# A 10-stage transformer kernel on one core: the first stage's norm factor is applied to the gate and up banks instead of to x, and two modulation groups move to the fourth feed-forward stage

## What is computed

```
def rmsnorm(x, g):
    x32 = x.astype(jnp.float32)
    y = x32 * lax.rsqrt(jnp.mean(x32 * x32, axis=-1, keepdims=True) + RMS_EPS)
    return (y * g.astype(jnp.float32)).astype(x.dtype)

def swiglu(x, w_in, w_out):
    gate, up = jnp.split(x @ w_in, 2, axis=-1)
    return (jax.nn.silu(gate) * up) @ w_out

x = x + 0.5 * swiglu(rmsnorm(x, ffn1_norm_g[l]), ffn1_w_in[l], ffn1_w_out[l])   # first stage
c_act = jax.nn.silu(c)
mod = c_act @ mod_w[i] + mod_b[i]                                               # 18 groups of 1024 columns
```

## Time and profile before

| | |
|---|---|
| median of 3 runs | 1636.75 us |
| the profiled execution | 1635.02 us |
| its span, first to last instruction | 1633.3 us (1.7 us lie outside) |
| PE busy | 1619.9 us, 99% |
| DVE busy | 1190.6 us, 73% |
| ACT busy | 802.6 us, 49% |
| mean granted TensorE clock | 0.996 |
| mean DMA rate over the span | 223 GB/s |

### The profile page before, as it was taken

How to read it: one execution, slowest core, us unless ns; L and a number is a source line. 1 busy time by engine, 2 the same in 40 slices (tenths; PEclk the granted TensorE clock), 3 DMA queues, 4 the chain that set the end, 5 groups by cost and what they waited for, 6 DMA issues and landing times.

```text
span 1633.3 us, 33769 instructions
## 1 busy us (share of the span) xinstructions
PE 1619.9 (99%) x14172; PEld 1592.6 (98%) x14172; DVE 1190.6 (73%) x1348; ACT 802.6 (49%) x887; POOL 48.1 (3%) x81
## 2 busy tenths in 40 slices
PE   9999999999999999999999999999999999999998
PEld 9999999999999999999999999999999998899998
DVE  6888876676788888888877788847655578774544
ACT  5444557554544445434457654445444456654442
POOL 0000000000000000000000000000000001000000
PEclk9999999999999999999999999999999999999999
DMA  8998845344489885988743368754555535445551
GB/s 334 340 335 322 309 155 181 137 159 154 172 299 327 325 331 192 329 332 296 271 155 130 141 222 323 268 194 151 203 203 183 202 130 185 152 155 195 192 192 65
DMA packets 51063, 365.02 MB, mean 223 GB/s; under 512 B 5792, under 2 KB 5920, under 8 KB 7072
## 3 DMA queue, kind: packets, MB, share of 16 engines
q1 hardware_dynamic: 40320, 287.04, 48.0%
q0 software_dynamic: 10368, 75.50, 12.9%
q10 hardware_dynamic: 288, 1.18, 0.2%
HBM read 362.65 MB, written 1.05 MB: 223 GB/s over the span
## 4 chain that ended last, share of the span: by engine, by line
PE 95%; DVE 3%; ACT 1%; issue 1%; DVEq 0%; ACTq 0%
PE bank L258 53%; PE bank L294 26%; PE bank L250 3%; PE bank L277 3%; PE bank L374 1%; PE bank L1817 1%; PE bank L385 1%; DVE wlo L189 1%; PE bank L2228 0%; PE bank L419 0%; PE bank L1324 0%; PE bank L1863 0%; PE bank L1769 0%; PE bank L1787 0%; PE bank L815 0%
## 5 line engine op out<-in xcount | busy, mean ns | idle before, releaser
L189 DVE TENSOR_TENSOR wlo<-raw,whi 128x2048 fp32r<-128x2048 f32 x253 | 578.7, 2288 | 220.0 <-ACT whi L181 219.8
L258 PE MATMUL bank<-xh,whi 128*128 128x256 f32 x2608 | 724.8, 278 | 0.7 <-DVE wlo L189 0.7
L258 PE MATMUL bank<-xl,whi 128*128 128x256 f32 x2608 | 721.4, 277 | 0.0
L258 PE MATMUL bank<-xh,wlo 128*128 128x256 f32 x2608 | 721.3, 277 | 0.0
L181 ACT ACTIVATE whi<-raw 128x2048 fp32r<-128x2048 f32 x253 | 483.6, 1914 | 308.0 <-PE bank L258 190.8
L258 PEld LDWEIGHTS bank<-xh,whi 128*128 128x128 f32 x2608 | 490.5, 188 | 2.2 <-DVE wlo L189 0.9
L258 PEld LDWEIGHTS bank<-xl,whi 128*128 128x128 f32 x2608 | 489.9, 188 | 0.1
L258 PEld LDWEIGHTS bank<-xh,wlo 128*128 128x128 f32 x2608 | 489.7, 188 | 0.0
L294 PE MATMUL bank<-hid_hi,whi 128*128 128x256 f32 x1056 | 291.9, 276 | 0.0
L294 PE MATMUL bank<-hid_hi,wlo 128*128 128x256 f32 x1056 | 291.5, 276 | 0.0
L294 PE MATMUL bank<-hid_lo,whi 128*128 128x256 f32 x1056 | 291.5, 276 | 0.0
(11 more groups left out here) (349 smaller groups left out, 1737.5 us busy)
## 6 DMA issues: line engine op xcount, KB each, us to landing
raw<-stream_in SPq DMA_DIRECT2D x269, 1024.0 KB, 4.9
mod_raw<-mod_in POOLq DMA_DIRECT2D x72, 1024.0 KB, 7.2
params<-params_in SPq DMA_DIRECT2D x1, 1474.0 KB, 14.3
x<-x_in SPq DMA_DIRECT2D x2, 512.0 KB, 4.5
raw<-stream_in SPq DMA_DIRECT2D x2, 512.0 KB, 6.6
m_gsu<-sgu_in ACTq DMA_DIRECT2D x1, 1024.0 KB, 6.9
y_out<-x SPq DMA_DIRECT2D x4, 256.0 KB, 2.6
consts<-consts_in SPq DMA_DIRECT2D x1, 280.5 KB, 6.3
```

Source lines behind the costliest of these rows:

```text
L189: dve.tensor_tensor(wlo[:, s, :], raw[:, s, :], whi[:, s, :].bitcast(F32), ALU.subtract)\
L258: last = pe.matmul(out[:, m, :], (whi, wlo)[wp][:, s, k * 256 + m * P:k * 256 + m * P + P], (xh, xl)[ap][:, k, :], start=(k == 0 and j == ...
```

## The change

Ffn 0 gets its own code (`FACTOR_LATER`). x is no longer multiplied by the norm's factor. ACT rounds x times gain for tiles 0 to 3, and DVE for tiles 4 to 7 (`xh`), as x lands, and DVE takes the remainders. Block 0 goes whi with xh, whi with xl, and wlo with xh last. Gate and up of step 0 go to two accumulator banks that are free then. The squares are summed behind block 1 by one matmul against ones (`pe_mean_squares`), which leaves the sum on all partitions. The root and the reciprocal are taken on 128x256 instead of 128x2. Each gate bank is multiplied by the factor on DVE (`scale_gate`) ahead of Silu, and each up bank likewise (first instruction of `post`), which are two more DVE instructions of 128x512 per step. The gains are loaded on ACT's queue, the masks are made later, and there are 78 dummy matmuls at the start instead of 70, and none in the first norm. `MOD_GROUPS` becomes 3, 5, 5, 5, and in ffn 0 the groups stand in turns 1 to 3 of 0 to 4. Some semaphores are merged, with no change to an order.

```
+FACTOR_LATER = (0,)
-MOD_GROUPS = {0: 5, 1: 5, 2: 5, 3: 3, 4: 0, 5: 0}
+MOD_GROUPS = {0: 3, 1: 5, 2: 5, 3: 5, 4: 0, 5: 0}
...
+                for k in range(4):
+                    act.activation(xh[:, k, :], x[:, k, :], ACT.Identity, scale=g[:, k:k + 1]).then_inc(sem("xn_rounded"), 2)
...
+        def dve_first_remainders(dve):
+            g = prm(GAIN_OF[0])
+            dve.wait_ge(sem("gain_loaded"), 16)
+            for k in range(2):
+                dve.wait_ge(sem("xn_rounded"), 2 * k + 2)
+                dve_remainder(dve, 0, k)
+            dve.wait_ge(sem("x_loaded1"), 16)
+            for k in range(4, 8):
+                dve.tensor_scalar(xh[:, k, :], x[:, k, :], g[:, k:k + 1], None, ALU.mult).then_inc(sem("xn_ready"), 1)
+                if k < 6:
+                    dve.wait_ge(sem("xn_rounded"), 2 * k - 2)
+                    dve_remainder(dve, 0, k - 2)
+            for k in range(4, 8):
+                dve.wait_ge(sem("xn_ready"), k - 3)
+                dve_remainder(dve, 0, k)
...
+        def dve_fold_squares(dve, n):
+            i = N_PAIRS * pair_index[n]
+            dve.wait_ge(sem("x_squared"), X_STEPS * norm_index[n] + X_STEPS)
+            for step, w in enumerate((4, 2, 1)):
+                if step:
+                    dve.wait_ge(sem("x_paired"), i + step)
+                dve.tensor_tensor(xm[:, 0:w, :], xm[:, 0:w, :], xm[:, w:2 * w, :], ALU.add)\
+                   .then_inc(sem("x_paired"), 1 if step < 2 else N_PAIRS - 2)
+        def pe_mean_squares(pe, n):
+            pe.wait_ge(sem("x_paired"), N_PAIRS * pair_index[n] + N_PAIRS)
+            pe.matmul(STAT[:, 0:T], ones, xm[:, 0, :], start=True, stop=True, skip_group_check=True).then_inc(sem("x_summed"), 1)
...
+        def pe_first_block(pe, out):
+            s = slot_of(0)
+            for part, (w, xs) in enumerate(((whi, xh), (whi, xl), (wlo, xh))):
+                if part == 2:
+                    pe.wait_ge(sem("w_lo_ready"), 1)
+                for k in range(KD):
...
+                    if part == 0 and k == 4:
+                        pe.wait_ge(sem("w_hi_ready"), 1)
+                    if part == 0:
+                        pe.wait_ge(sem("xn_rounded" if k < 4 else "xn_ready"), 2 * k + 2 if k < 4 else k - 3)
+                    if part == 1:
+                        pe.wait_ge(sem("xn_split"), k + 1)
+                    for m in range(2):
...
+        def pe_ffn_later(pe, n, f, groups):
...
+                pe_first_block(pe, pair(ACC[0]))
...
+            pe_in(pe, F0 + 1, pair(ACC[1]))
+            pe_mean_squares(pe, n)
+            def turn(i, first):
+                for q in range(2):
+                    b = F0 + 2 + 3 * q
+                    if not (first and q == 0):
+                        pe.wait_ge(sem("bank_scaled"), L0 + 1 + 2 * q + 4 * i)
+                    pe_in(pe, b, pair(GATE), i, 6)
+                    if first and q == 0:
...
+                        pe_apart(pe, STAT[:, 0:P])
+                    else:
+                        pe.wait_ge(sem("bank_scaled"), L0 + 2 + 2 * q + 4 * i)
+                    pe_in(pe, b + 1, pair(UP), i, 6)
+                    pe.wait_ge(sem("hid_split"), S0 + 1 + q + 2 * i)
+                    pe_out(pe, b + 2, hid_hi[:, q], hid_lo[:, q], first and q == 0, False, i, 6)
...
+            pe_out(pe, F0 + 32, hid_hi[:, 0], hid_lo[:, 0], False, True, between=lambda: pe_mod_fold(pe, n, f, groups))
...
+        def act_ffn_later(act, n, f):
...
+            act_rounded_gain(act, n)
+            if n == 0:
+                act.wait_ge(sem("w_loaded_part"), 16)
+                act.activation(whi[:, 0, 0:H], raw[:, 0, 0:H], ACT.Copy).then_inc(sem("w_half_ready"), 1)
+                act.wait_ge(sem("w_loaded0"), 16)
+                act.activation(whi[:, 0, H:BLK], raw[:, 0, H:BLK], ACT.Copy).then_inc(sem("w_hi_ready"), 1)
+                act_squares(act, 0)
+                act_split(act, 1)
+                act.wait_ge(sem("x_loaded1"), 16)
+                act_squares(act, 1)
+                act_split(act, 2)
...
+            act_split(act, F0 + 3)
+            act_root(act, n)
+            act_split(act, F0 + 4)
+            def silu(s, i=0, ps=0):
+                act.wait_ge(sem("bank_scaled"), L0 + 2 * s + 1 + 2 * ps * i)
+                act.activation(gate[:, :, :], gate[:, :, :], ACT.Silu).then_inc(sem("silu_done"), 1)
...
+            silu(0)
+            round_hidden(0, 0)
...
+            def turn(i, first):
+                for q in range(2):
+                    b = F0 + 2 + 3 * q
+                    if not (first and q == 0):
+                        act_split(act, b + 2, i, 6)
+                    act_split(act, b + 3, i, 6)
+                    silu(1 + q, i, 2)
+                    round_hidden(1 + q, (1 + q) % 2, i, 2)
+                    act_split(act, b + 4, i, 6)
...
+            dve_split(dve, F0 + 3)
+            dve_factor(dve, n)
+            def scale_gate(s, src, block, i=0, per=0, ps=0):
+                dve.wait_ge(sem("w_used"), block + 1 + per * i)
+                if s > 0:
+                    dve.wait_ge(sem("hid_ready"), S0 + s + ps * i)
+                dve.tensor_tensor(gate[:, :, :], src, over(rstd[:, :], [P, 2, T]), ALU.mult).then_inc(sem("bank_scaled"), 1)
+            def post(s, src, block, parity, i=0, per=0, ps=0, between=None):
+                dve.wait_ge(sem("w_used"), block + 1 + per * i)
+                if s > 0:
+                    dve.wait_ge(sem("hid_split"), S0 + s + ps * i)
+                dve.tensor_tensor(hid[:, :, :], src, over(rstd[:, :], [P, 2, T]), ALU.mult).then_inc(sem("bank_scaled"), 1)
+                dve.wait_ge(sem("bank_scaled"), L0 + 2 * s + 2 + 2 * ps * i)
+                dve.wait_ge(sem("silu_done"), S0 + s + 1 + ps * i)
+                dve.tensor_tensor(hid[:, :, :], hid[:, :, :], gate[:, :, :], ALU.mult).then_inc(sem("hid_ready"), 1)
+                if between is not None:
+                    between()
+                dve.wait_ge(sem("hid_rounded"), S0 + s + 1 + ps * i)
+                dve.tensor_tensor(hid_lo[:, parity], hid[:, :, :], hid_hi[:, parity].bitcast(F32), ALU.subtract)\
+                   .then_inc(sem("hid_split"), 1)
+            scale_gate(0, pair(ACC[0]), F0)
+            post(0, pair(ACC[1]), F0 + 1, 0, between=lambda: dve_split(dve, F0 + 4))
...
+            def turn(i, ahead, with_mod, first=False):
...
+                for q in range(2):
+                    b, step = F0 + 2 + 3 * q + 6 * ahead, 1 + q + 2 * ahead
+                    if with_mod:
+                        mod_block(2 * q, g0, i)
+                    if not (first and q == 0):
+                        dve_split(dve, b + 2, i, 6)
+                    scale_gate(step, pair(GATE), b, i, 6, 2)
+                    if with_mod:
+                        mod_block(2 * q + 1, g0, i)
+                    dve_split(dve, b + 3, i, 6)
+                    post(step, pair(UP), b + 1, (1 + q) % 2, i, 6, 2)
+                    dve_split(dve, b + 4, i, 6)
+                    if with_mod and q == 1:
+                        mod_sum(g0, i)
+            turn(0, 0, False, True)
+            with dve.Fori(0, groups) as i:
+                turn(i, 1, True)
...
-            sp.dma_start(params[:, 0:4 * KD], a_params[:, 0:4 * KD]).then_inc(sem("consts_loaded"), 16)
...
-            for _ in range(70):
+            for _ in range(78):
...
+            act.dma_start(params[:, 0:4 * KD], a_params[:, 0:4 * KD]).then_inc(sem("gain_loaded"), 16)
...
-            for p in range(N_PAIRS):
-                dve_pair(dve, 0, p)
...
```

More of the change, by code:

```diff
@@ L412, in pe_norm @@
             if n == 0:
-                pe.wait_ge(sem("consts_loaded"), 32)
+                pe.wait_ge(sem("consts_loaded"), 16)
                 pe.wait_ge(sem("masks_ready"), 3)
@@ L487, in build_program @@
         pair_index = {n: i for i, n in enumerate(n for n in norm_index if n != AFTER_FINAL)}
+        spread_index = {n: i for i, n in enumerate(n for n in norm_index if n not in FACTOR_LATER)}
+        later_index = {n: i for i, n in enumerate(FACTOR_LATER)}
         split_index = {}
@@ L577, in pe_ffn @@
             pe.wait_ge(sem("hid_split"), S0 + STEPS)
-            pe_out(pe, F0 + 32, hid_hi[:, 0], hid_lo[:, 0], False, True, between=mod_fold if groups else None)
+            pe_out(pe, F0 + 32, hid_hi[:, 0], hid_lo[:, 0], False, True, between=(lambda: pe_mod_fold(pe, n, f, groups)) if groups else None)
+        def pe_first_block(pe, out):
[3 more added lines that the diff above has]
+                    pe.wait_ge(sem("w_lo_ready"), 1)
+                for k in range(KD):
+                    if part == 0 and k == 0:
+                        pe.wait_ge(sem("w_half_ready"), 1)
+                    if part == 0 and k == 4:
[5 more added lines that the diff above has]
+                    for m in range(2):
+                        c = k * 256 + m * P
```

(40 more changed lines are left out.)

145 lines of the change are left out of this document (117 added, 28 removed).

## The result

The changed kernel took 1636.43 us, the median of 22 executions (1633.03 to 1642.89), against 1634.92 (1631.47 to 1636.94) of the kernel before. The ratio is 1.0016, 95% interval 1.0009 to 1.0024: 2.6 us slower, which is measurable but inside the 0.2% that I called no change. That closeness is part luck: my number was the kernel before plus 0.15, with 1636.75 for the kernel before, the median of 3 executions, and over 22 that median is 1.8 us lower. The executions do not lie round it, though. With 12 more from a later comparison, 23 of 34 lie between 1633.0 and 1638.2 (median 1636.0) and 11 between 1640.2 and 1643.4 (median 1641.8), with nothing between. The kernel before shows no such second level: its highest in these two comparisons (22 and 35 executions) is 1639.6.

The account below looks back on a forecast made before the run. PE, busy 1619.9 of 1633.3 us, bounds the kernel. Block 4 -0.2, landings -0.2, end of ffn 0 -0.15, end of ffn 3 +0.7 make +0.15 on 1635.02; with 1.73 to the median, 1636.9 us, no change, range 1635.0 to 1639.2.

Parts of the forecast that it names:

- Up to block 3: Start of ffn 0: block 1 at about 17.2, block 2 ending 3.4 us earlier, block 3 at 30.67, gain 1.3 us.
- The landings: DMA queues at the start: moving the gains to ACT's queue lands weights earlier, 0.2 us gained, bounds 0 and 0.5.
- Block 4: First output block: step 0's longer chain lets PE start it at 37.3 against 37.51, 0.2 us gained.
- DVE's turns: First stage: a turn with a group takes 34.3 us against PE's 32.64; the reserve covers it, cost 0.
- Ends of stages: Column sums: end of ffn 0 gains 0.15 us, end of ffn 3 loses 0.7.
- From there on PE works without a break in both kernels: From block 4 on: PE never waits as long as DVE keeps up.
- Rival B: Pauses ahead of blocks 3 and 4, and ffn 3's end: the clock falls, 1638 to 1639.6 us; chance 0.18.

Follow-up runs that it names:

- experiment 3: The changed kernel with 32 small matmuls in place of one between block 2 and block 3, filling PE's first pause: 1636.36 us, ratio 1.0014.
- experiment 5: The changed kernel with GpSimd's first two modulation loads waiting for block 3's landing, and groups 4, 5, 5, 4 in place of 3, 5, 5, 5: 1640.01 us.
- experiment 1: The changed kernel with one more small matmul ahead of each of output blocks 4 and 7, behind PE's wait for hid_split: 1636.11 us, ratio 1.0006.
- experiments 1 to 4: experiment 1, experiment 3, experiment 4, and the changed kernel with GpSimd's first two modulation loads waiting for block 3's landing, 1631.57 us.
- experiment 7: The kernel before, with PE waiting ahead of block 4 for DVE's fourth multiply-add and a stray matmul ahead of block 5: 1637.07 us, ratio 1.0010.
- experiment 6: The kernel before, with PE waiting ahead of block 4 also for DVE's fourth modulation multiply-add: 1638.67 us, ratio 1.0028.
- experiment 4: The kernel before, with only the modulation groups moved (3, 5, 5, 5 in place of 5, 5, 5, 3): 1635.00 us, ratio 1.0003.
- experiment 12: The changed kernel, GpSimd's first two modulation loads behind block 3's landing, one stray matmul between the first two blocks of five later feed-forward stages: 1632.47 us.

## Why the prediction was right, and where it was not

**Up to block 3: right.** Block 1 started at 17.0 to 17.7 (forecast 17.2), block 3 at 30.7 to 31.2 (30.67) behind a pause of 1.65 to 1.75 us (2.1). The weights' landing was the gate. Block 2 ended 2.7 to 3.3 us earlier than before (forecast 3.4), and block 3 started only 0.8 to 1.3 us earlier.

**The landings: wrong sign.** I took 0.2 us for an earlier landing. ACT began to round block 3 at 26.4 to 26.9 in four profiles of the changed start, and at 25.8 to 26.7 in four of the old start: 0.4 later on the mean, with overlapping ranges. What made it later is open. The sentence beside the term (the Trainium skill, Trainium Kernel Development and Optimization, Key Constraints: issuing from several engines saves only issue time) would have made it 0, nearer than mine.

**Block 4: chain right, 0.3 late.** Table load, Silu, remainder and `hid_lo` follow as listed. Without a fall and in the fast rhythm (experiment 3) block 4 starts at 37.62, against 37.51 before and my 37.3.

**DVE's turns: right.** 34.46 us by the trace, 34.3 forecast, and no wait of PE for DVE between 40 and 190 us. The reserve was smaller than I thought in one respect: I worked out 1.7 us after turn 3 for the remainders, and experiment 5 showed that the next group also hits `hid_lo` and the fold.

**Ends of stages: right.** ffn 0's sums took 2.19 us (forecast 2.26), ffn 3's 2.94 (2.94).

**The sum for the lower level.** Block 4 +0.1 to 0.3 (`hid_lo` was done at 37.5 to 37.8 in the four profiles), end of ffn 0 -0.3, end of ffn 3 +0.7: +0.5 to +0.7 where I had +0.15. The lower level's median, 1636.0, is 0.7 to 1.0 over the two medians of before.

**"From there on PE works without a break in both kernels": true, and the step that failed.** I took from it that PE also works at the same pace, 5.44 us a block. In 11 of 34 executions it was 5.65. By the levels' medians that is 5.8 us in a third of the executions, 1.9 on the mean, of the 2.7 and 3.1 us by which the means of the two comparisons differ. Rival B had the place, the pauses, and the event, a fall in block 3, but priced only the clock, at up to 2.7, and not the rhythm that PE kept behind it. The clock did fall in block 3 in both profiles of the unedited change and cost little, 1.9 us in block 3 of which the wait ahead of block 4 takes back 1.1. The rule of the Trainium skill that I set against B (TensorE: Matmul & The Clock Gate, Part 1: a fall only after a stretch with no work) would have left it out; the trace has the fall 1.1 us behind a pause of 1.74, in a stretch with PE busy on both sides.

So the number 1636.9 came out near the median because its base, 1.8 us too high, stood in for the slow rhythm, 1.9 us on the mean, which the sum did not have.

What stays open: why a restart or a return of the clock takes the one rhythm or the other, and why a stray matmul in the flow changes it, mostly to the fast one. The runs show when it happens, not the mechanism in PE. How many of the upper executions had a fall of the clock too, and whether the change would have its upper level without the fall, isn't known, as only two were profiled and both had it.

## What to carry to other kernels

When a stage starts earlier, follow the next thing it needs back through every queue, and ask which other loads may stand back: here 2.1 MB stood in the way that were first used at 61.7 us, 35 us behind the block that they held up, and moving them turned a change of +2.6 us into one of -1.8 to -2.8. A short pause of a saturated TensorE can cost far more than its length: look at matmuls per microsecond at full granted clock, not only at busy time. And look at all executions, not at the median: two levels point to a state that a single profile may or may not show.

## What the runs showed of the hardware

TensorE ran streams of 128x256 matmuls with weight loads at 113.3 or at 117.8 ns each, at the same granted clock of 1.00 (2.4 GHz), and kept one rhythm for up to 160 us. The slow one was seen behind a restart at full clock, out of a wait of 1.65 us (experiment 1, block 3) and of 0.7 to 0.9 us (block 1 in experiments 1 to 4, but not in 7 other profiles). In both profiles of the unedited change it set in across a fall of the clock, and behind a like fall in experiment 7 it lasted half a us. The times show the upper level in 11 of 34 executions of the change and 4 of 12 of experiment 6. One small matmul of another shape in the running flow brought the fast one back (54.90 us in experiment 1, 32.30 us in experiment 4); directly behind a pause it did not (37.65 us in experiment 1), at one place of a mixer it did not in any profile (271.70 us in the kernel before), and once, in experiment 12, it ended a fast one. The same two rhythms stand in the profiles of the kernel before, at the stages' starts: 11.30 us for two blocks at 1139.12, 5.50 for one behind the stray matmul. There it costs 0.4 us.
